# A hybrid layer on one core: attention's result carried by channels into gate and out projection

## The chip, the cores and the metric

The kernel runs on one core of a Trainium2 chip. The metric is the device time of one execution in microseconds (us), given as the median of the runs made on the same chip. All matrices and all arithmetic are float32.

## What is computed

Two layers follow each other on 2048 tokens of width 1024. The first one, which the change is in, is a hybrid: one wide input projection feeds a sliding-window attention (8 query heads, 2 key heads of width 64, blocks of 128 queries against 256 keys, one sink per head), an RWKV7 mixer and a gated linear attention (GLA). The three results, each times its gate, go side by side through one out projection. The second layer (top-k attention, pooling) is left out here; the change doesn't touch it.

```
s = einsum('bnqhgd,bnkhd->bnhgqk', qb, kb) * D ** -0.5 - slopes * dist     # masked
p = softmax(concatenate([s, sink], axis=-1), axis=-1)[..., :-1]
attn = einsum('bnhgqk,bnkhd->bnqhgd', p, vb) * silu(ag)
...
y = concatenate([attn, rwkv, gla], axis=-1) @ w_out
return x + gate[:, None] * rms_norm(y, g_post)
```

## The kernel before

The kernel has four stages, one after the other. Two of them matter here.

**First projections** (up to about 806 us). A loop over the 16 tiles of 128 tokens multiplies the normed tile by the columns of `w_in`. A helper `channels` gives a result with channels on the partitions (weights as the stationary side, 128 columns at a time), `tokens` one with tokens on the partitions (the tile as the stationary side, up to 512 columns at a time). The gate of attention, "ag", is the last product of a tile: `tokens(B[7], C_AG, 512)` at L380. ACT and DVE turn it into a gate and SP stores it with the rest of the tile. Its weights come by two DMAs (L215, `fetch_weights("ag", ...)`), those of the queries by 16 small ones (L211), which pick each head's 64 columns.

**Mixers** (about 808 to 1540 us, the `mixers` function, names with `b_`). A software pipeline over a pass number `p`: in one pass, tile `a = p + 1` gets its scores, attention, GLA and the inverse of RWKV's triangular matrix, tile `b = p` RWKV's state, tile `o = p - 1` the out projection (`dense`, in eight pieces), and `c = p + 2` its preparation. Each engine has its own list of steps, written out by hand in the loop at the end of its block, and goes through it strictly in order; waits are on semaphores. A ring of four PSUM banks is handed from user to user in the order of `bank_users`.

The steps that the change and the prediction speak of, for tile `a`:

- PE `scores` (L1047), two pairs of heads; DVE `biased` (L1470) adds the distance bias and keeps a maximum for each head; DVE `maxima` (L1477, L1478).
- ACT `probabilities` (L1260): eight exponentials with their sums in `den`, then the sinks' (L1263).
- PE `turn_probs` 0 to 3 (L1055) transposes two heads each, ACT and DVE copy them to `pT`; PE `attend` (L1065) multiplies by the values, which gives the result by channels, still not divided.
- ACT `take_attended` (L1273) copies it, PE `turn_attended` (L1072) transposes it to tokens by channels, DVE `attended` (L1518) divides it by `den` (whose `denominators`, L1511 and L1512, add the sink and take the reciprocal), POOL `attention_gate` (L836) multiplies by the gate.
- One pass later PE `turn_y` (L933) transposes all of `y` back to channels by tokens for the out projection: `turn_y(o, 1)` RWKV's and GLA's half, `turn_y(o, 0)` attention's; DVE (L1457) and ACT (L1209) copy them to `yT`; PE `dense` (L1115) multiplies.

Beside them run the five rounds of RWKV's inverse: PE `Z` (L979), ACT `take_Z` (L1219), PE `XY_products` (L989, L992), DVE `join_X` (L1429) and `join_Y` (L1433). DVE's `next_state` (L1447, L1450) makes the state that PE's `state_products` (L1011) reads. DVE's `gla_near` (L1483, L1495) takes GLA's first blocks out of the four ring banks; DVE's `out_sum` (L1562) finishes a tile of output. POOL's `level_distances` (L794), `key` (L773 to L775) and `bonus_terms` (L781, L782) prepare tile `c`; they begin when that tile's DMA has landed.

## Time and profile before

| | us |
|---|---|
| Median of 3 runs | 3612.84 |
| Lowest and highest | 3610.74, 3613.15 |
| The profiled execution | 3611.44 |
| Span of its trace | 3609.7 |

| Engine | busy us | share of the span |
|---|---|---|
| PE (matmul) | 3497.7 | 97% |
| PEld (weight load) | 2660.5 | 74% |
| DVE | 1910.8 | 53% |
| ACT | 1585.6 | 44% |
| POOL | 417.0 | 12% |

The span leaves out what lies before the first and behind the last instruction, here 1.7 us. An engine's busy share is taken over four stages that have different limits, so a stage's own rows decide. The granted clock of TensorE was 0.992 over the span.

### The profile page before, as it was taken

To read this page: it belongs to the slowest core of one execution; us is meant where nothing else is said; L and a number is where in the kernel's file an instruction comes from. 1 tells how busy PE (TensorE), PEld (TensorE's weight loads), DVE (VectorE), ACT (ScalarE), POOL (GpSimd) and SP (SyncE) were. 2 spreads that over 40 slices of the span, in tenths; PEclk is the share of its full clock that TensorE was granted. 3 is DMA by queue.
4 is the path that set the end of the run, shared out by engine and by line. 5 is a ranking of instruction groups with operands and counts; after the bars stand their busy time and mean duration, and the time that the engine had idled before them with its cause. 6 is when DMAs were issued, how large, how long until landed. Compare 5 with 4: busy or idle time off the path is not lost. (4 is left out here: it accounts for less than half of the span.)

```text
span 3609.7 us, 69211 instructions
## 1 busy us (share of the span) xinstructions
PE 3497.7 (97%) x28060; PEld 2660.5 (74%) x28060; DVE 1910.8 (53%) x4800; ACT 1585.6 (44%) x3591; POOL 417.0 (12%) x689
## 2 busy tenths in 40 slices
PE   6999999997999999989999999999999999999998
PEld 5887788766666666578778887777886677777765
DVE  5223333247777777534788788666683343333322
ACT  2223233323444444313677666777753344443320
POOL 0000000005444444310000000000000000000000
PEclk9999999998999999999999999999999999999999
DMA  9111111123222222241111114121215212111121
GB/s 314 54 54 48 54 54 54 54 86 147 84 77 81 76 76 76 90 132 48 50 54 62 53 52 168 56 66 60 69 46 194 74 53 78 42 49 67 48 84 41
DMA packets 134963, 282.05 MB, mean 78 GB/s; under 512 B 26640, under 2 KB 86048, under 8 KB 127136
## 3 DMA queue, kind: packets, MB, share of 16 engines
q1 hardware_dynamic: 125968, 267.75, 21.0%
q0 software_dynamic: 2304, 8.39, 0.6%
q8 instruction: 192, 3.15, 0.4%
q10 hardware_dynamic: 6416, 2.08, 0.2%
q14 instruction: 83, 0.68, 0.1%
HBM read 181.72 MB, written 96.47 MB: 77 GB/s over the span
## 5 line engine op out<-in xcount | busy, mean ns | idle before, releaser
L2575 ACT ACTIVATE at_pT<-at_bank 128x512 f32<-128x512 f32 (+3 forms) x320 | 154.4, 531 | 535.1 <-PE at_bank L2474 534.8
L1976 PEld LDWEIGHTS p_bank<-p_hT,w_in_rest 128*128 128x128 f32 x3072 | 345.5, 192 | 14.5 <-issue 12.4
L1976 PE MATMUL p_bank<-p_hT,w_in_rest 128*128 128x128 f32 x3072 | 350.2, 276 | 1.6 <-DVE p_st L2256 1.3
L2097 ACT ACTIVATE p_r<-p_acc,p_mid 128x384 f32<-128x384 f32 (+13 forms) x224 | 292.9, 1308 | 58.8 <-DVE p_acc L2283 54.4
L306 PE MATMUL p_bank<-p_hT,w_in_rest 128*128 128x128 f32 x2080 | 267.3, 275 | 0.0
L1115 PE MATMUL b_banks<-b_wout,b_yT 128*128 128x512 f32 x512 | 248.0, 610 | 3.7 <-DVE b_yT L1457 2.2
L306 PEld LDWEIGHTS p_bank<-p_hT,w_in_rest 128*128 128x128 f32 x2080 | 249.9, 192 | 0.0
L2515 PE MATMUL at_bank<-arena,at_y 128*128 128x512 f32 x512 | 239.8, 599 | 4.1 <-DVE at_y L2625 2.5
L1967 PE MATMUL p_bank<-arena,p_hT 128*128 128x512 f32 (+2 forms) x768 | 241.9, 467 | 1.3 <-ACT p_hT L2091 1.3
L2155 ACT ACTIVATE p_r<-p_bank,ahead_rows 128x512 f32<-128x512 f32 (+3 forms) x304 | 167.9, 635 | 156.5 <-PE p_bank L2070 144.5
L2058 PE MATMUL p_bank<-p_hTg,arena 128*128 128x256 f32 x1024 | 226.7, 381 | 1.7 <-ACT arena L2119 1.7
L2058 PE MATMUL p_bank<-p_hTg,w_in_rest 128*128 128x256 f32 x1024 | 228.2, 381 | 0.0
L2271 DVE SCALAR_TENSOR_TENSOR p_acc<-p_r,ahead_rows,p_acc 128x512 f32<-128x512 f32 (+3 forms) x266 | 166.9, 681 | 108.0 <-ACT p_r L2155 105.7
L2058 PEld LDWEIGHTS p_bank<-p_hTg,w_in_rest 128*128 128x128 f32 x1024 | 192.7, 190 | 42.0 <-issue 15.9
L2058 PEld LDWEIGHTS p_bank<-p_hTg,arena 128*128 128x128 f32 x1024 | 193.2, 190 | 39.6 <-issue 13.2
L2596 DVE CUSTOM_DVE_ANT_0 at_s<-at_bank,at_bias 128x512 f32<-128x512 f32 (+3 forms) x312 | 173.4, 608 | 71.9 <-PE at_bank L2461 67.8
L1967 PEld LDWEIGHTS p_bank<-arena,p_hT 128*128 128x128 f32 x768 | 142.3, 191 | 89.4 <-issue 69.1
L312 PE MATMUL p_bank<-w_in_rest,p_hT 128*128 128x512 f32 (+2 forms) x640 | 202.3, 463 | 0.0
L2289 DVE TENSOR_SCALAR_CACHE_REDUCE p_tie<-p_acc,p_mid 128x384 f32<-128x384 f32 (+13 forms) x126 | 186.3, 1479 | 14.7 <-ACT p_mid L2099 10.7
L306 PE MATMUL p_bank<-p_hT,arena 128*128 128x128 f32 x1248 | 175.6, 276 | 4.5 <-ACT p_hT L400 2.9
L312 PEld LDWEIGHTS p_bank<-w_in_rest,p_hT 128*128 128x128 f32 x640 | 110.4, 190 | 82.8 <-issue 76.5
L2439 POOL DMA_DIRECT2D out<-at_o x16 | 8.8, 549 | 1395.1 <-DVE at_o L2635 1395.1
(419 smaller groups left out, 6240.6 us busy)
## 6 DMA issues: line engine op xcount, KB each, us to landing
stage<-p_st SPq DMA_DIRECT2D x15, 1856.0 KB, 5.9
arena<-stage SPq DMA_DIRECT2D x15, 1856.0 KB, 7.5
at_rest<-stage SPq DMA_DIRECT2D x16, 1280.0 KB, 5.9
stage<-p_pr SPq DMA_DIRECT2D x128, 128.0 KB, 1.8
p_ada<-in_ada_w SPq DMA_DIRECT2D x8, 1024.0 KB, 9.2
p_xt<-in_x SPq DMA_DIRECT2D x16, 512.0 KB, 3.2
b_x<-in_x SPq DMA_DIRECT2D x16, 512.0 KB, 3.2
x<-b_x SPq DMA_DIRECT2D x16, 512.0 KB, 3.1
```

The lines of the kernel that those rows point to most:

```text
L306: last = mm(out, w_in(k, place(c), place(c) + P), hT[:, k, 1:P + 1], start=(k == 0), stop=(k == KD - 1))
L312: last = mm(out, hT[:, k, 1:P + 1], w_in(k, place(c), place(c) + width), start=(k == 0), stop=(k == KD - 1))
L1115: last = mm(OUT[:, :], yT[:, k, :], wout[:, k, half * 512:(half + 1) * 512], start=(k == 0), stop=(k == KD - 1))
L1967: last = mm(bank[:, 0:width], hTs[:, n % 2, k, :], weights(k, c, c + width), start=(k == 0), stop=(k == KD - 1))
L1976: last = mm(bank[:, m * P:(m + 1) * P], weights(k, c + m * P, c + (m + 1) * P), hTs[:, n % 2, k, :], start=(k == 0), stop=(k == KD - 1))
L2058: last = mm(gate_bank[:, 0:2 * P], weights(k, c, c + P), hTg[:, g % 2, k, :], start=(k == 0), stop=(k == KD - 1))
L2097: ch.link(f(flat(r[:, :, :])[:, 0:L], acc[:, slot.buf_a, 0:L], ACT.Sign, scale=-1.0, bias=m, accum_out=tally[:, 0:1]))
L2155: f(r[:, q, 0:width_], FRONT[q][:, 0:width_], ACT.Relu, scale=wi[:, slot.a, head:head + 1]).then_inc(S["relu_done"], 1)
L2271: last = stt(part, r[:, q, 0:width_], sgn, part, ALU.mult, ALU.add)
L2289: ch.link(ts(tie[:, 0:L], acc[:, slot.buf_b, 0:L], m[:, 0:1], 0.0, ALU.is_ge, ALU.add, accum_out=cnt[:, 0:1]))
L2515: last = mm(bank[:, :], y[:, k, :], wo[:, k, half * 512:(half + 1) * 512], start=(k == 0), stop=(k == KD - 1))
L2596: v.tensor_tensor_reduce(out=s[:, step % 2, g, at:at + w], in0=FRONT[2 * (j % 2) + g][:, 0:w], in1=bias_of(n)[:, at:at + w], scale=HEAD ** ...
```

## The change

Attention's result stays with channels on the partitions from `attend` to the out projection.

- `take_attended` writes it into `ys` as it is; POOL multiplies it there by a gate that now also has channels on its partitions; `dense` reads that half of its stationary side from `ys`. `turn_attended`, `turn_y(o, 0)`, ACT's copy of it and DVE's `attended` are gone. `dense` waits for attention's gate at its first piece and for the copy of the other half at its third.
- For this the gate "ag" is projected by `channels`, four times 128 columns, in the order in which heads lie in the attention's result. Its weights come by 16 DMAs like the queries', and the rows of `w_out` in the same order.
- The division moves to the probabilities: `denominators` now stands behind `gla_near`, ahead of `join_X(a, 1)`, and multiplies all of `s` by the reciprocals in two operations of 128 x 1024 elements each (for tile 0, 128 x 512). `turn_probs` waits for the first of them (0 and 1) or the second (2 and 3) instead of for ACT's exponentials.
- Around it: `maxima` goes ahead of `out_sum`; the first four exponentials go ahead of `take_Z(a, 1)`; `state_products(b, 1)` goes ahead of `turn_probs` 2 and 3; the ring has 26 users a pass instead of 28; for tile 0, `level_exps` and `scaled_levels` stand a little later.

```diff
@@ -212,7 +212,11 @@
...
                 sp.dma_start(xt[:, :], A["x"][0][P:2 * P, :]).then_inc(S["x_loaded"], 16)
-                fetch_weights("ag", (C_AG, C_RKV))
+                at = place(C_AG)
+                for k in range(KD):
+                    for g in range(A_KV):
+                        sp.dma_start(w_in(k, at, at + 512).rearrange("p (c g d) -> p g c d", g=2, d=HEAD)[:, g],
+                                     wsrc[:, k, C_AG + 256 * g:C_AG + 256 * g + 256].rearrange("p (c d) -> p c d", d=HEAD)).then_inc(S["ag_weights"], 16)
                 sp.wait_ge(S["first_added"], 2)
@@ -300,10 +304,11 @@
...
 
-                    def channels(out, c):
-
+                    def channels(out, c, more=0):
+
+                        at = place(c) + more
                         for k in range(KD):
-                            last = mm(out, w_in(k, place(c), place(c) + P), hT[:, k, 1:P + 1], start=(k == 0), stop=(k == KD - 1))
+                            last = mm(out, w_in(k, at, at + P), hT[:, k, 1:P + 1], start=(k == 0), stop=(k == KD - 1))
                         return last
@@ -378,8 +383,10 @@
...
                             last.then_inc(S["summed"], 1)
-                    pe.wait_ge(S["ag_weights"], 32)
-                    tokens(B[7][:, :], C_AG, 512).then_inc(S["ag_proj"], 1)
+                    pe.wait_ge(S["ag_weights"], 16 * A_KV * KD)
+                    for c in range(4):
+                        last = channels(B[7][:, c * P:(c + 1) * P], C_AG, c * P)
+                    last.then_inc(S["ag_proj"], 1)
 
@@ -680,9 +687,9 @@
...
             a, b, o = p + 1, p, p - 1
-            uses = [("x4t1", a), ("x4t0", a), ("yt1", o), ("yt0", o), ("gram0", a), ("gram1", a)] + [(f"score{i}", a) for i in range(4)]
+            uses = [("x4t1", a), ("x4t0", a), ("yt1", o), ("gram0", a), ("gram1", a)] + [(f"score{i}", a) for i in range(4)]
             uses += [("gla0", a)] * 4 + [(f"prob{i}", a) for i in range(4)] + [("rwkv", b), ("cum", p + 2), ("attT", a)] + [("gla1", a)] * 4
-            uses += [("ke", a), ("gout", a), ("att", a)]
+            uses += [("ke", a), ("gout", a)]
             bank_users += [(name, n) for name, n in uses if valid(n)]
@@ -727,7 +734,9 @@
...
                 wsrc = A["w_out"][0].rearrange("(k p) n -> p k n", p=P)
-                for k in range(0, KD, 2):
+                for g in range(A_KV):
+                    sp.dma_start(wout[half_of(g), 0:4, :], A["w_out"][0][256 * g:256 * g + 256, :].rearrange("(c d) n -> d c n", d=HEAD)).then_inc(S["wout_loaded"], 16)
+                for k in range(KD // 2, KD, 2):
                     sp.dma_start(wout[:, k:k + 2, :], wsrc[:, k:k + 2, :]).then_inc(S["wout_loaded"], 16)
@@ -830,7 +839,7 @@
...
                     y = ys[:, n % 3, 0:512]
-                    pool.wait_ge(S["att_taken"], n + 1)
+                    pool.wait_ge(S["attT_taken"], n + 1)
                     if n == 0:
@@ -922,16 +931,13 @@
...
 
-                def turn_y(n, e):
-                    if e == 0:
-                        pe.wait_ge(S["att_gated"], n + 1)
-                    else:
-                        pe.wait_ge(S["scaled_gla"], n + 1)
-                        pe.wait_ge(S["y_ready"], n + 1)
-                    bank = bank_for(f"yt{e}", n)
+                def turn_y(n):
+                    pe.wait_ge(S["scaled_gla"], n + 1)
+                    pe.wait_ge(S["y_ready"], n + 1)
+                    bank = bank_for("yt1", n)
                     for k in range(4):
-                        last = tr(bank[:, k * P:(k + 1) * P], ys[:, n % 3, (4 * e + k) * P:(4 * e + k + 1) * P], ident[:, :])
-                    last.then_inc(S[f"yt{e}_done"], 1)
+                        last = tr(bank[:, k * P:(k + 1) * P], ys[:, n % 3, (4 + k) * P:(5 + k) * P], ident[:, :])
+                    last.then_inc(S["yt1_done"], 1)
 
@@ -1048,7 +1054,7 @@
...
                 def turn_probs(n, j):
-                    pe.wait_ge(S[f"probs{j}"], n + 1)
+                    pe.wait_ge(S[f"probs{j // 2}"], n + 1)
                     bank = bank_for(f"prob{j}", n)
@@ -1064,13 +1070,6 @@
...
                     last.then_inc(S["attT_done"], 1)
-
-                def turn_attended(n):
-                    pe.wait_ge(S["attT_taken"], n + 1)
-                    bank = bank_for("att", n)
-                    for i in range(4):
-                        last = tr(bank[:, i * P:(i + 1) * P], flat(s[:, 0:2, :])[:, i * P:(i + 1) * P], ident[:, :])
-                    last.then_inc(S["att_done"], 1)
 
@@ -1105,14 +1104,16 @@
...
                     if piece == 0:
-                        for e in range(2):
-                            pe.wait_ge(S[f"yt{e}_taken"], n + 1)
+                        pe.wait_ge(S["att_gated"], n + 1)
                         if n == 0:
...
                         from_one(pe, S["r_taken"], 2 * n + half)
+                    if piece == 2:
+                        pe.wait_ge(S["yt1_taken"], n + 1)
                     for k in range(2 * (piece % 4), 2 * (piece % 4) + 2):
-                        last = mm(OUT[:, :], yT[:, k, :], wout[:, k, half * 512:(half + 1) * 512], start=(k == 0), stop=(k == KD - 1))
+                        part = ys[:, n % 3, k * P:(k + 1) * P] if k < 4 else yT[:, k - 4, :]
+                        last = mm(OUT[:, :], part, wout[:, k, half * 512:(half + 1) * 512], start=(k == 0), stop=(k == KD - 1))
                     if piece % 4 == 3:
@@ -1125,8 +1126,7 @@
...
                     if valid(o):
-                        turn_y(o, 1)
-                        turn_y(o, 0)
+                        turn_y(o)
                     if valid(a):
@@ -1154,11 +1154,11 @@
...
                         turn_probs(a, 1)
+                    if valid(b):
+                        state_products(b, 1)
+                    if valid(a):
                         turn_probs(a, 2)
                         turn_probs(a, 3)
-                    if valid(b):
-                        state_products(b, 1)
-                    if valid(a):
                         XY_products(a, 2)
@@ -1188,7 +1188,6 @@
...
                     if valid(a):
-                        turn_attended(a)
                         update_and_weights(a)
@@ -1202,11 +1201,6 @@
...
                         f(X4Ts[:, n % 2, 2 * e:2 * e + 2, :, :].rearrange("p a b c -> p (a b c)"), RING[spot_of[f"x4t{e}", n] % 4], ACT.Copy).then_inc(S[f"x4t{e}_taken"], 1)
-
-                def turned_y(n):
-                    act.wait_ge(S["yt0_done"], n + 1)
-                    from_one(act, S["out_done"], 2 * n)
-                    f(flat(yT[:, 0:4, :]), bank_of("yt0", n), ACT.Copy).then_inc(S["yt0_taken"], 1)
 
@@ -1250,16 +1244,13 @@
...
 
-                def probabilities(n, j):
-                    if j == 2:
-                        act.wait_ge(S["max_ready"], n + 1)
-                        from_one(act, S["att_taken"], n)
+                def exponentials(n, g):
+                    act.wait_ge(S["max_ready"], n + 1)
+                    from_one(act, S["probs1"], n)
                     first = 0 if n else P
-                    for e in range(2):
-                        h = 4 * (j % 2) + 2 * (j // 2) + e
-                        last = f(s[:, h, first:], s[:, h, first:], ACT.Exp, bias=nm[:, h:h + 1], accum_out=den[:, h:h + 1])
-                    last.then_inc(S[f"probs{j}"], 1)
-                    if j == 3:
+                    for h in range(4 * g, 4 * g + 4):
+                        f(s[:, h, first:], s[:, h, first:], ACT.Exp, bias=nm[:, h:h + 1], accum_out=den[:, h:h + 1])
+                    if g == 1:
                         f(am[:, :], am[:, :], ACT.Exp).then_inc(S["sink_exp"], 1)
@@ -1270,7 +1261,8 @@
...
                     act.wait_ge(S["attT_done"], n + 1)
-                    f(flat(s[:, 0:2, :]), bank_of("attT", n), ACT.Copy).then_inc(S["attT_taken"], 1)
+                    from_one(act, S["out_done"], 2 * (n - 2))
+                    f(ys[:, n % 3, 0:512], bank_of("attT", n), ACT.Copy).then_inc(S["attT_taken"], 1)
 
@@ -1310,20 +1302,17 @@
...
                 decays(0)
-                level_exps(0)
                 for p in range(-1, TILES + 1):
...
                         turned_X4(a)
-                    if valid(o):
-                        turned_y(o)
+                    if a == 0:
+                        level_exps(a)
                     if valid(a):
                         first_X(a)
+                        exponentials(a, 0)
                         take_Z(a, 1)
-                        probabilities(a, 2)
-                        probabilities(a, 0)
-                        probabilities(a, 1)
-                        probabilities(a, 3)
+                        exponentials(a, 1)
                     if valid(o):
@@ -1462,7 +1451,6 @@
...
                         from_one(dve, S["sink_exp"], n)
-                        from_one(dve, S["att_done"], n)
                     first = 0 if n else P
@@ -1510,13 +1498,11 @@
...
                     ch.link(v.reciprocal(den[:, :], den[:, :]))
-
-                def attended(n):
-                    dve.wait_ge(S["att_done"], n + 1)
-                    from_one(dve, S["yt0_done"], n - 2)
-                    by_pair = lambda ap: ap.rearrange("p (g i d) -> p i g d", g=2, d=HEAD)
-                    tt(by_pair(ys[:, n % 3, 0:512]), bank_of("att", n).rearrange("p (i g d) -> p i g d", g=2, d=HEAD),
-                       spread(den[:, :].rearrange("p (g i) -> p i g", g=2).unsqueeze(3), [P, 4, 2, HEAD]), ALU.mult).then_inc(S["att_taken"], 1)
+                    first = 0 if n else P
+                    for i in range(2):
+                        by_group = s[:, :, first:].rearrange("p (g i e) t -> p i g e t", g=2, i=2)[:, i]
+                        share = spread(den[:, :].rearrange("p (g i e) -> p i g e", g=2, i=2)[:, i].unsqueeze(3), [P, 2, 2, 2 * P - first])
+                        tt(by_group, by_group, share, ALU.mult).then_inc(S[f"probs{i}"], 1)
 
@@ -1565,7 +1551,6 @@
...
                 bonus(0)
-                scaled_levels(0)
                 dve.wait_ge(S["setup_done"], 1)
@@ -1575,20 +1560,22 @@
...
                         take_grams(a)
+                        if a == 0:
+                            scaled_levels(a)
                         biased(a, 0)
                         biased(a, 1)
+                        maxima(a)
                     if valid(o - 1):
...
                     if valid(a):
-                        maxima(a)
                         gla_near(a)
+                        denominators(a)
                         join_X(a, 1)
...
                         turned_probs(a, 1)
-                        denominators(a)
                     if valid(b):
@@ -1624,7 +1611,6 @@
...
                     if valid(a):
-                        attended(a)
                         gla_scale(a)
...
```

DVE, in the full pass for tile 2 of the mixers, from `gla_near` on (before):

```order
L1483 TENSOR_TENSOR b_gA<-b_banks,ident 128x512
L1495 COPY_PREDICATED b_gA<-b_g_masks,b_banks 128x256
L1495 COPY_PREDICATED b_gA<-b_g_masks,b_banks 128x128x2
L1495 COPY_PREDICATED b_gA<-b_g_masks,b_banks 128x64x4
L1429 TENSOR_TENSOR b_XY<-b_XY,b_banks 128x256
L1447 SCALAR_TENSOR_TENSOR b_dM<-b_banks,b_pend,b_pair 128x128 x2
L1450 SCALAR_TENSOR_TENSOR b_M<-b_M,b_pend,b_dM 128x128 x2
L1433 TENSOR_TENSOR b_XY<-b_XY,b_banks 128x256
L1507 COPY b_pT<-b_banks 128x512
L1511 TENSOR_TENSOR b_den<-b_den,b_am 128x8
L1512 RECIPROCAL b_den<-b_den 128x8
L1438 SCALAR_TENSOR_TENSOR b_SA<-b_banks,b_U 64x256
```

The same place after the change (L1471 and L1483 are `gla_near`, L1505 the two wide multiplications, L1418 `join_X`, L1436 and L1439 `next_state`, L1422 `join_Y`):

```order
L1471 TENSOR_TENSOR b_gA<-b_banks,ident 128x512
L1483 COPY_PREDICATED b_gA<-b_g_masks,b_banks 128x256
L1483 COPY_PREDICATED b_gA<-b_g_masks,b_banks 128x128x2
L1483 COPY_PREDICATED b_gA<-b_g_masks,b_banks 128x64x4
L1499 TENSOR_TENSOR b_den<-b_den,b_am 128x8
L1500 RECIPROCAL b_den<-b_den 128x8
L1505 TENSOR_TENSOR arena<-arena,b_den 128x2x512 x2
L1418 TENSOR_TENSOR b_XY<-b_XY,b_banks 128x256
L1436 SCALAR_TENSOR_TENSOR b_dM<-b_banks,b_pend,b_pair 128x128 x2
L1439 SCALAR_TENSOR_TENSOR b_M<-b_M,b_pend,b_dM 128x128 x2
L1422 TENSOR_TENSOR b_XY<-b_XY,b_banks 128x256
L1495 COPY b_pT<-b_banks 128x512
```

`denominators` and the two wide operations have moved from behind the copy of the probabilities to ahead of `join_X`, `next_state` and `join_Y`.

PE, the same pass, from the fourth piece of `dense` to the second round's products (before):

```order
L1115 MATMUL b_banks<-b_wout,b_yT 128x512 x2
L1055 MATMUL b_banks<-ident,arena 128x128 x4
L979 MATMUL b_banks<-b_XY,b_cT 64x64 x8
L1055 MATMUL b_banks<-ident,arena 128x128 x12
L1011 MATMUL b_banks<-b_M,b_WT 64x128 x2
L989 MATMUL b_banks<-b_Z,b_XY 64x64 x8
```

The same place after (L1116 is `dense`, L1061 `turn_probs`, L985 `Z`, L1017 `state_products`, L995 and L998 the products):

```order
L1116 MATMUL b_banks<-b_wout,b_yT 128x512 x2
L1061 MATMUL b_banks<-ident,arena 128x128 x4
L985 MATMUL b_banks<-b_XY,b_cT 64x64 x8
L1061 MATMUL b_banks<-ident,arena 128x128 x4
L1017 MATMUL b_banks<-b_M,b_WT 64x128 x2
L1061 MATMUL b_banks<-ident,arena 128x128 x8
L995 MATMUL b_banks<-b_Z,b_XY 64x64 x8
L998 MATMUL b_banks<-b_XY,b_Z 64x64 x8
```

The state's products stand between the second and the third group of transposes, so that these have four transposes before and eight behind them instead of twelve before.

## Rows read from the trace of the kernel before

**Rows 1.** The mixers' stage by windows: length, busy us of each engine (instructions), TensorE clock

```profile
850.00:1500.00 650.00, 640.68 (x8857) 440.94 (x8857) 478.95 (x1265) 272.09 (x988) 303.92 (x447) 1.00 0.21 73
```

**Rows 2.** Timeline of PE, one full pass: start, length, line, operation, count [idle before]

```profile
1196.07 1.04 PE L922 MATMUL b_banks<-ident,b_X 128*128 128x128 f32 x8
...
1197.62 1.09 PE L933 MATMUL b_banks<-ident,b_y 128*128 128x128 f32 x8
...
1213.90 0.60 PE L1055 MATMUL b_banks<-ident,arena 128*128 128x128 f32 x4
1214.43 0.68 PE L979 MATMUL b_banks<-b_XY,b_cT 64*64 64x64 f32 x16
1215.04 1.53 PE L1055 MATMUL b_banks<-ident,arena 128*128 128x128 f32 x12
1216.51 0.65 PE L1011 MATMUL b_banks<-b_M,b_WT 128*64 128x128 f32 x4
1217.09 0.68 PE L989 MATMUL b_banks<-b_Z,b_XY 64*64 64x64 f32 x16
...
1236.46 0.60 PE L1072 MATMUL b_banks<-ident,arena 128*128 128x128 f32 x4
...
1239.65 1.04 PE L922 MATMUL b_banks<-ident,b_X 128*128 128x128 f32 x8
```

**Rows 3.** Timeline of PE, first projections, one tile

```profile
404.97 0.83 PE L306 MATMUL p_bank<-p_hT,arena 128*128 128x128 f32 x6
...
406.75 0.83 PE L306 MATMUL p_bank<-p_hT,arena 128*128 128x128 f32 x6
...
414.20 2.74 PE L312 MATMUL p_bank<-arena,p_hT 128*128 128x512 f32 x6
...
421.07 0.83 PE L306 MATMUL p_bank<-p_hT,arena 128*128 128x128 f32 x6
```

**Rows 4.** Timeline of DVE, the same pass as rows 2

```profile
1192.03 1.08 DVE L1404 TENSOR_TENSOR b_gql<-b_ge,arena 128x896 f32<-128x896 f32 x1
...
1209.22 0.69 DVE L1483 TENSOR_TENSOR b_gA<-b_banks,ident 128x512 f32<-128x512 f32 x1 [0.72 <-PE b_banks L1085]
1209.95 1.97 DVE L1495 COPY_PREDICATED b_gA<-b_g_masks,b_banks 128x256 f32<-128x256 uint32 x3
1212.27 0.42 DVE L1429 TENSOR_TENSOR b_XY<-b_XY,b_banks 128x256 f32<-128x256 f32 x1 [0.34 <-PE b_banks L992]
...
1213.24 1.10 DVE L1450 SCALAR_TENSOR_TENSOR b_M<-b_M,b_pend,b_dM 128x128 f32<-128x128 f32 x2
...
1216.35 0.16 DVE L1511 TENSOR_TENSOR b_den<-b_den,b_am 128x8 f32<-128x8 f32 x1
```

**Rows 5.** Timeline of ACT, the same pass

```profile
1208.54 0.51 ACT L1260 ACTIVATE arena<-arena,b_nm 128x256 f32<-128x256 f32 x1
...
1212.49 0.19 ACT L1263 ACTIVATE b_am<-b_am 128x8 f32<-128x8 f32 x1
```

**Rows 6.** Timeline of POOL, the same pass

```profile
1207.65 2.64 POOL L794 TENSOR_TENSOR b_ge<-arena 128x128 f32<-128x128 f32 x7 [1.92 <-DMA arena<-stage]
1210.26 0.72 POOL L773 TENSOR_TENSOR arena<-arena,ahead_rows 128x256 f32<-128x256 f32 x1
...
1213.47 0.73 POOL L782 TENSOR_TENSOR arena<-arena,ahead_rows 128x256 f32<-128x256 f32 x1
```

**Rows 7.** Timeline of all engines, the last passes of the mixers

```profile
1503.93 0.61 POOL L818 TENSOR_TENSOR b_t<-b_late,b_bonus 128x256 f32<-128x256 f32 x1
1504.06 1.57 DVE L1562 SCALAR_TENSOR_TENSOR b_x<-b_r,b_osum,b_x 128x1024 f32<-128x1024 f32 x1 [0.73 <-issue]
...
1504.62 1.58 POOL L819 TENSOR_TENSOR b_t<-b_t,b_rows 128x256 f32<-128x256 f32 x1
...
1524.21 7.11 PE L1115 MATMUL b_banks<-b_wout,b_yT 128*128 128x512 f32 x16 [1.27 <-DVE b_yT L1457]
```

**Rows 8.** Timeline of SP's queue, first projections

```profile
59.34 6.27 SPq L211 DMA_DIRECT2D w_in_rest<-in_w_in  x10
```

8 lines of the change are left out of this document (4 added, 4 removed).

## The prediction

> **What bounds the kernel now.** I read the stages first. In the mixers PE is busy 640.7 of 650 us at full clock, DVE 479, POOL 304 [rows 1], and in the timeline of one full pass PE's rows stand without a bracket of idle time, from one pass start at 1196.07 to the next at 1239.65, 43.58 us [rows 2]. So there PE's own work sets the time, and any wait put into it adds in full. The first projections look the same: the rows of one tile follow each other without a bracket [rows 3]. What has to be found is what PE loses in work, and whether something that PE reads now comes after PE wants it. For the second I read DVE, ACT and POOL in the same pass [rows 4 to 6]. All times of day below are those of this pass.
>
> **What PE loses and gains.** Four transposes before `Z` of round 2 take 1214.43 - 1213.90 = 0.53 us, the twelve behind it 1216.51 - 1215.04 = 1.47, so 0.49 for four; `turn_y` has eight, and its row has 1.09 [rows 2]. `turn_attended` (four, at 1236.46) and half of `turn_y` (four, at 1197.62) go: about 1.03 us a pass, the first 0.5 of it near the pass's start. The out projection keeps its multiplications, only half of its operand is read elsewhere: nothing.
>
> The gate "ag" by tokens takes 421.07 - 414.20 = 6.87 us; a block of 128 channels takes 406.75 - 404.97 = 1.78, four take 7.12 [rows 3]. That is +0.25 us a tile, **+4.0** for 16 tiles, all of it on PE's path.
>
> The 16 small loads of its weights: ten such loads held SP's queue for 6.27 us [rows 8], 0.63 each, so 16 take 10 us where two were. Behind them on SP are the loads of the ada weights and the next x tile. The gate is the last product of the first tile and the query loads went ahead of it in the same way; I take 0 and keep 0 to 5 us (half of the 10) for the range.
>
> ACT loses a copy and DVE a multiplication of 512 elements from PSUM; neither is on the path. POOL's gate waited for DVE's division, now for ACT's copy, which is earlier; it has other work in front of it in its list, so nothing.
>
> **What DVE gets ahead of PE's next step.** `Z` of round 2 started at 1214.43 and needs `join_X` of round 1, which ran from 1212.27 to 1212.69: 1.74 us of slack [rows 2, 4]. After the change PE wants it 0.5 earlier, at 1213.93, and DVE does this first:
>
> - `gla_near` began at 1209.22, released by PE, and ended at 1209.95 + 1.97 = 1211.92 [rows 4]. It moves with PE: 1208.7 to 1211.4. The sinks' exponential is no hindrance: ACT needed 1208.54 to 1212.68 for all [rows 5] and starts about 1.6 us earlier, since `maxima` no longer stands behind `out_sum` (1.57 us, of which 0.48 is waiting, in [rows 7]) and PE is 0.5 ahead.
> - the sum and the reciprocal of `den`: the first has 0.16 [rows 4], the second and the two semaphores between them I put at 0.25: 0.4, to about 1211.85.
> - two wide multiplications. No row has this operation on 1024 elements with both inputs in SBUF; the nearest is 1.08 us for 896 [rows 4], scaled 1.2, with 1.15 from start to start. Together 2.3, the bounds are 2.0 and 2.6.
> - `join_X`, 0.42.
>
> If nothing else interferes, `join_X` begins at 1214.15 and ends at 1214.55, and `Z` is 0.65 late. The state follows: `next_state` (0.6 and two operations of `L1450`, 0.65 when free) would be ready at 1215.8, the state's products, now moved ahead, begin then, 0.58 and eight transposes (0.98) later comes round 2's first product at 1217.4 instead of 1217.09. That is +0.35 against the gain of 0.5 that should have been there, and with `turn_attended` gone the pass is 0.15 us **shorter**.
>
> **The pair of engines.** It won't be free, I think. POOL runs `level_distances` from 1207.65, when the tile's DMA lands, and then five multiplications of 256 elements, the first at 1210.26, the last at 1213.47 to 1214.20, each 0.72, 0.80 apart [rows 6]. What happens when DVE and POOL both read two operands from SBUF stands in three places. `L1450`, two operations on 128 elements, took 1.10 us under POOL's last one and ended at 1214.34, 0.14 behind it [rows 4, 6]. In the last passes `L1562` (1024 elements, DVE) was issued at 1504.06 within a POOL operation that ended at 1504.54; it ended at 1505.63, 1.09 behind it. The POOL operation issued at 1504.62 took 1.58 and ended 0.57 behind DVE's [rows 7]. One waits for the other, and they take turns.
>
> The Trainium skill has this as a rule (SBUF — State Buffer, Who interferes with whom): a tensor_tensor on VectorE with both inputs in SBUF and a GpSimd instruction that reads SBUF exclude each other, and the second one fully blocks. By the rows the later one loses a little less than its full length; by the rule taken to the letter both wide operations and the POOL operations beside them pay in full, some 0.5 us more a pass, and the time would be about 3637 as an estimate by that page.
>
> With turns taken by the rows: POOL's five operations come 0.5 later, like the gate on which its DMA waits, at 1210.8, 1211.6, 1212.4 and on. The first wide operation, issued at 1211.85, waits until 1212.3 and ends 1.09 later at 1213.4; POOL's third ends at 1213.95; the second wide one at 1215.05; `join_X` runs 1215.0 to 1215.4. `Z` waits from 1213.93 to 1215.4, **1.5 us**. Then `L1447` to 1215.9, `L1450` behind POOL's fifth until 1216.85; the state's products begin at 1216.9; round 2's product 1.56 later, at 1218.45. Against 1217.09 that is +1.35, less 0.5 for `turn_attended`: **+0.8 us a pass**. The transposes themselves aren't what waits: the first wide result is there at 1213.4, PE wants it at 1213.4.
>
> **Sum.** Tiles 2 to 14 have a full pass with POOL's preparation: 13 x 0.8 = +10.4. Tile 15 has no tile to prepare: -0.15. Tile 1 has no out projection beside it that covers DVE's chain, so all of the inserted 2.7 and a collision or two land there, less 0.5: +3. Tile 0 has half the width: +1.5. In the last two passes the out projection waited for the copies, once for 1.27 us [rows 7]; now it can begin without them: -1.6 with the transposes. The gate's projection +4.0. Together +17.2 on the profiled 3611.4, that is 3628.6; the median of the runs shown stands 1.4 above that execution: **3630 us**.
>
> **The rivals.**
>
> - *No collision*: POOL is through, or DVE gets the pair between POOL's operations without loss. Per pass -0.15, tile 1 +2, tile 0 +1, last passes -1.6, gate +4.0: +3.3, so 3616. For it: the start of POOL's five hangs on a DMA, and 0.5 us of slip is my inference. Against: they cover 3.9 us, and a shift of one microsecond either way still meets a wide operation.
> - *Faster*: PE waits for none of it. Then 16 x 1.03 = 16.5 goes, 4.0 comes: 3600. The place is `Z` of round 2, and the price is DVE's 2.7 us in front of `join_X`. It decides the other way only if that chain starts 0.65 us earlier than I have it (and the pair is free); `gla_near` is released by PE's GLA products, which the change moves only with all the rest. Little speaks for it but the wide operations being shorter than 0.9 each, which the 1.08 for 896 elements denies.
> - *Dearer*: collisions also on `den` itself, full lengths, and the first tile's weights late. 1.5 a pass x 13 = 19.5, with tile 0 and 1 +5, gate +4, weights +4, tail -1.6: +31, so 3644.
> - *The gate's cost is hidden or the order of weights costs nothing* changes 4 us at most and none of the above.
>
> **Chances.** Forecast with collisions 0.5, no collision 0.22, dearer 0.13, faster 0.15. The range 3608 to 3643 takes in the second and most of the third. A difference of 0.2% (7.2 us) is about what a measurement of this kernel can tell from none: faster by that only in the fourth case, 0.15; the no-collision case lies within it, 0.22; the rest is slower, 0.63.
>
> **What the profile of the changed kernel would show.** PE in a full pass: a bracket of 1 to 2 us ahead of `Z` of round 2, released by DVE's `join_X`, and a smaller one ahead of the state's products; no bracket ahead of `turn_probs`. Pass length 44.4 (43.4 without collisions, 42.5 if the faster case holds). DVE: the wide operations at 1.5 to 1.9 us each instead of 1.2, `L773`'s successors on POOL longer than 0.72. First projections: a tile 0.25 longer. I am wrong if the wide operations show 1.2 us and PE still waits, if the bracket stands at `turn_probs` (then ACT's sums are the late part), or if the transposes were not worth 0.5 each.

## The result and the profile after

| | before | after |
|---|---|---|
| Median | 3612.99 us (4 runs) | 3653.39 us (4 runs) |
| Lowest and highest | 3610.74, 3613.18 | 3648.51, 3654.25 |
| The profiled execution | 3611.44 | 3653.63 |
| Span of its trace | 3609.7 | 3651.8 |

The ratio is 1.0112 [1.0099, 1.0125]: 40 us slower. The sign of the prediction held, the size did not: 17 us were forecast, and the range ended at 3643.

```profile
850.00:1500.00 650.00, 610.27 (x8293) 412.13 (x8293) 485.94 (x1216) 253.17 (x927) 311.32 (x425) 0.97 0.20 72
```

PE is busy 30 us less than in [rows 1] and its mean clock is 0.97, so PE both waits more and runs slower in part of the time. What PE waits for between 900 and 1500 us (line and what it waited for, us in total, times, longest):

```profile
PE b_banks L985 <- DVE b_XY L1418: 18.0, 14, 1.3
PE b_banks L1017 <- DVE b_M L1439: 6.5, 13, 0.8
PE b_banks L1061 <- DVE arena L1505: 1.7, 6, 0.3
```

The first is `Z` of round 2, the second the state's products, the third `turn_probs`. Timeline of PE in one full pass, the answer to [rows 2]:

```profile
1183.72 1.04 PE L931 MATMUL b_banks<-ident,b_X 128*128 128x128 f32 x8
...
1199.29 1.98 PE L1116 MATMUL b_banks<-b_wout,b_yT 128*128 128x512 f32 x4
1201.59 0.66 PE L1061 MATMUL b_banks<-ident,arena 128*128 128x128 f32 x4 [0.32 <-DVE arena L1505]
1203.58 0.68 PE L985 MATMUL b_banks<-b_XY,b_cT 64*64 64x64 f32 x16 [1.34 <-DVE b_XY L1418]
1204.20 0.66 PE L1061 MATMUL b_banks<-ident,arena 128*128 128x128 f32 x4
1205.15 0.62 PE L1017 MATMUL b_banks<-b_M,b_WT 128*64 128x128 f32 x4 [0.29 <-DVE b_M L1439]
1205.70 1.09 PE L1061 MATMUL b_banks<-ident,arena 128*128 128x128 f32 x8
1206.72 0.68 PE L995 MATMUL b_banks<-b_Z,b_XY 64*64 64x64 f32 x16
```

Three brackets stand where [rows 2] has none. Timeline of DVE in the same pass ([rows 4] before):

```profile
1196.43 0.69 DVE L1471 TENSOR_TENSOR b_gA<-b_banks,ident 128x512 f32<-128x512 f32 x1 [0.82 <-PE b_banks L1084]
1197.16 1.96 DVE L1483 COPY_PREDICATED b_gA<-b_g_masks,b_banks 128x256 f32<-128x256 uint32 x3
1199.15 0.52 DVE L1499 TENSOR_TENSOR b_den<-b_den,b_am 128x8 f32<-128x8 f32 x1
...
1199.95 3.25 DVE L1505 TENSOR_TENSOR arena<-arena,b_den 128x1024 f32<-128x1024 f32 x2
1203.12 0.41 DVE L1418 TENSOR_TENSOR b_XY<-b_XY,b_banks 128x256 f32<-128x256 f32 x1
...
1204.09 0.91 DVE L1439 SCALAR_TENSOR_TENSOR b_M<-b_M,b_pend,b_dM 128x128 f32<-128x128 f32 x2
```

Timeline of POOL in the same pass ([rows 6] before):

```profile
1198.92 0.73 POOL L782 TENSOR_TENSOR arena<-arena,ahead_rows 128x256 f32<-128x256 f32 x1
1199.73 0.72 POOL L783 TENSOR_TENSOR arena<-arena,b_rows 128x256 f32<-128x256 f32 x1
1200.53 1.59 POOL L784 TENSOR_TENSOR arena<-arena 128x256 f32<-128x256 f32 x1
1202.20 1.59 POOL L790 TENSOR_TENSOR arena<-arena 128x256 f32<-128x256 f32 x1
```

The two take turns, as forecast. `L783` holds the pair until 1200.45. The first wide operation, issued at 1199.95, ends at about 1201.55 (an estimate: `turn_probs`, which waits for it, starts at 1201.59); `L784` ends at 1202.12, the second wide one near 1203.2, `L790` at 1203.79. Each DVE operation ends 1.1 us behind POOL's, each POOL operation 0.57 behind DVE's, the two numbers of [rows 7]. The Trainium skill's exclusive lock (SBUF — State Buffer, Who interferes with whom) fits this in its order, and in the rows the one that waited ends 0.1 to 0.2 us less than its full length behind the other (DVE's takes 1.22 alone, POOL's 0.73).

Now the clock, in the pass that follows, in windows of the changed kernel:

```profile
1240.00:1250.00 10.00, 8.33 (x110) 4.99 (x106) 8.94 (x14) 5.46 (x22) 7.62 (x12) 1.00 0.40 141
1250.00:1254.00 4.00, 3.44 (x26) 2.81 (x28) 2.55 (x5) 0.06 (x1) 0.27 (x1) 0.60 0.00 0
1254.00:1258.00 4.00, 4.00 (x86) 3.40 (x82) 2.11 (x7) 0.71 (x2) 0.85 (x1) 0.97 0.00 0
```

and PE's timeline there:

```profile
1248.46 0.68 PE L985 MATMUL b_banks<-b_XY,b_cT 64*64 64x64 f32 x16 [1.34 <-DVE b_XY L1418]
...
1250.56 0.82 PE L1017 MATMUL b_banks<-b_M,b_WT 128*64 128x128 f32 x4 [0.83 <-DVE b_M L1439]
1251.31 1.97 PE L1061 MATMUL b_banks<-ident,arena 128*128 128x128 f32 x8
1253.21 1.12 PE L995 MATMUL b_banks<-b_Z,b_XY 64*64 64x64 f32 x16
```

After the waits the clock falls to the lower level, and the eight transposes take 1.97 us instead of 1.09. That pass lasts 46.95 us, its neighbours about 45. The wait for the state is 0.83 us here and was 0.29 in the pass above; it is 0.83 in every third pass or so, where `L1439` takes 1.45 us beside POOL.

**Where the 42.2 us between the profiled executions are**, by the starts of the passes (PE's first transposes of a pass, as at the top of [rows 2]):

| | before | after | difference | forecast |
|---|---|---|---|---|
| The first pass of the mixers starts at | 816.55 | 820.74 | +4.2 | +4.0 |
| Tile 0 | 35.69 | 42.93 | +7.2 | +1.5 |
| Tile 1 | 37.11 | 42.69 | +5.6 | +3 |
| Tile 2 | 45.24 | 48.90 | +3.7 | +0.8 |
| Tiles 3 to 14 | 12 x 43.58 | 547.2 | +24.2 | +9.6 |
| From tile 15's start to the next stage | 90.2 | 88.7 | -1.4 | -1.75 |
| The second layer | | | -1.3 | 0 |

Of the twelve passes eight last 44.6 to 45.6 us and four, with the lower clock in them, 46.2 to 47.1. At 45.0 each, +1.4 a pass, they make 17.0; the other 7.2 belong to the four with the clock. Of these some 5.5 are the clock itself: three of the four had the long wait for the state too, and the one pass with the same waits and no fall took 45.59, where they took 46.95 to 47.06.

### The profile page after: what moved, and what is told of

Its sections match the earlier page's. It is cut to its first block and busy times, and to the rows that moved or that the text cites. A ratio compares the mean times of both kernels' runs of the same rounds, so it can differ in the third digit from the quotient of the medians.

```text
span 3651.8 us, 70471 instructions
## 1 busy us (share of the span) xinstructions
PE 3509.4 (96%) x28700; PEld 2722.1 (75%) x28700; DVE 1942.3 (53%) x4816; ACT 1575.4 (43%) x3575; POOL 439.4 (12%) x689
## 5 line engine op out<-in xcount | busy, mean ns | idle before, releaser
L1962 PEld LDWEIGHTS p_bank<-p_hT,w_in_rest 128*128 128x128 f32 x3072 | 345.4, 192 | 14.0 <-issue 12.4
L1962 PE MATMUL p_bank<-p_hT,w_in_rest 128*128 128x128 f32 x3072 | 349.9, 276 | 1.3 <-DVE p_st L2242 1.3
L311 PE MATMUL p_bank<-p_hT,w_in_rest 128*128 128x128 f32 x2720 | 349.2, 275 | 0.0
L311 PEld LDWEIGHTS p_bank<-p_hT,w_in_rest 128*128 128x128 f32 x2720 | 326.4, 192 | 0.0
L311 PE MATMUL p_bank<-p_hT,arena 128*128 128x128 f32 x1632 | 228.9, 276 | 4.3 <-ACT p_hT L407 2.9
L311 PEld LDWEIGHTS p_bank<-p_hT,arena 128*128 128x128 f32 x1632 | 204.7, 192 | 8.0 <-issue 4.7
L2460 PEld LDWEIGHTS at_bank<-ident,at_s 128*128 128x128 f32 x1088 | 126.0, 141 | 43.9 <-issue 37.2
L2621 DVE TENSOR_TENSOR at_o<-at_bank,at_o 128x512 f32<-128x512 f32 x32 | 22.1, 692 | 252.3 <-PE at_bank L2501 252.3
```

The costliest lines, as they stand in the source:

```text
L311: last = mm(out, w_in(k, at, at + P), hT[:, k, 1:P + 1], start=(k == 0), stop=(k == KD - 1))
L1962: last = mm(bank[:, m * P:(m + 1) * P], weights(k, c + m * P, c + (m + 1) * P), hTs[:, n % 2, k, :], start=(k == 0), stop=(k == KD - 1))
L2460: last = tr(TURNED[j % 2][:, e * P:(e + 1) * P], s[:, step % 2, g, at + e * P:at + (e + 1) * P], ident[:, :])
```

## Experiments

The numbers of passes are those of tile 0, tile 1, tile 2 and one full pass. Before has 35.69, 37.11, 45.24 and 43.58 us, the changed kernel 42.93, 42.69, 48.90 and 44.6 to 47.1. They come from one profiled execution of each kernel. Full passes of one kernel without a fall of the clock lie within about 1 us of each other, in most versions within 0.5; tile 0 varies more, as two kernels below show whose edits first act in a later pass: with the changed kernel's program for tile 0, one took 40.16 us for it and the other 43.93.

### POOL out of the way

```diff
                         level_distances(c)
+                        if valid(b):
+                            pool.wait_ge(S["M_ready"], 2 * b + 1)
                         key(c)
```

> The changed kernel, with POOL's key and bonus of the next tile made to wait until DVE's next_state of the first chunk is done, so that no POOL operation stands beside the two wide multiplications. If the collisions between DVE and POOL stretch them (theory): the wide operations take 1.2 us each instead of 1.4 to 1.8, PE's wait ahead of the second Z falls from 1.3 to about 0.7 us, a full pass takes 43.6 to 43.9 us instead of 45.1 to 47.0, and the time is about 3627 us (3633 if TensorE's clock still falls in some passes). If the wide operations are slow by themselves (rival: the broadcast operand): they stay at 1.6 to 1.8 us and the time at 3653.

Measured: 3625.85 us, ratio 1.0043 [1.0026, 1.0060]; passes 40.16 (tile 0, which the edit doesn't reach), 40.6, 45.52 and 43.6 to 43.8, at full clock from tile 2 on. DVE's timeline in a full pass:

```profile
1225.27 2.36 DVE L1507 TENSOR_TENSOR arena<-arena,b_den 128x1024 f32<-128x1024 f32 x2
1227.54 0.41 DVE L1420 TENSOR_TENSOR b_XY<-b_XY,b_banks 128x256 f32<-128x256 f32 x1
```

and PE's, the only bracket left there:

```profile
1228.01 0.68 PE L987 MATMUL b_banks<-b_XY,b_cT 64*64 64x64 f32 x16 [0.78 <-DVE b_XY L1420]
```

The wide operations alone take 2.36 us for the pair (2.3 was the estimate), with POOL beside them 3.25. The collisions and what they bring in clock are worth some 26 of the 40 us, of which up to 2.8 may be tile 0's scatter.

### Without the wide operations

```diff
...
-                        tt(by_group, by_group, share, ALU.mult).then_inc(S[f"probs{i}"], 1)
+                        v.tensor_copy(nm[:, 4 * i:4 * i + 4], den[:, 4 * i:4 * i + 4]).then_inc(S[f"probs{i}"], 1)
```

> The changed kernel without the two wide multiplications: the probabilities stay undivided, two copies of four elements stand in their place, and the result isn't divided at all. Theory: PE's waits in the full passes go, a pass takes 42.6 us, no pass has the clock at half, and the time is about 3606 us; that would confirm the 1.03 us a pass that the transposes were worth. Rival (the waits come from other parts of the new order, such as maxima or the state's products ahead of the transposes): passes stay above 44 us and the time above 3630.

Measured: 3612.77 us, ratio 1.0003 [0.9994, 1.0013]; passes 40.04, 40.33, 45.14 and 42.9 to 43.1. So the 40 us go with the two wide operations, and even with the division free the change gives nothing. A full pass gains 0.5 to 0.7 us instead of 1.03, and tiles 0 and 1 lose 4.3 and 3.2 us with no wide operation in them.

### Is it the wait that lowers the clock?

```diff
                         turn_probs(a, 0)
+                        if valid(o):
+                            for _ in range(9):
+                                tr(ZB[:, 0:P], ident[:, :], ident[:, :])
                         Z(a, 2)
```

> The changed kernel with nine transposes of the identity into an unused part of Z's bank put on PE ahead of the second Z in each full pass, about 1.1 us of work in a wait of 1.3. Their result is overwritten. Theory (the falls of TensorE's clock in some passes come from PE's wait there): the passes of 47 us turn into 45.1, none has the clock at half, time about 3644 us. Rival (the clock falls for another reason, or the filler only adds to the path): 3653 us or more.

Measured: 3646.91 us, ratio 1.0099 [1.0082, 1.0116]; full passes 44.6 to 45.6, none with the lower clock. PE's waits:

```profile
PE b_banks L1017 <- DVE b_M L1442: 6.2, 12, 0.8
PE b_banks L985 <- DVE b_XY L1421: 5.2, 14, 0.5
```

DVE's part is as in the changed kernel, only PE does useless work in the wait, and the passes above 46 us are gone. One run without falls is unlikely to be luck: three other kernels below have the waits of the changed one in their full passes ("The start of tile 0 as before", "The gate by tokens", the changed kernel with plain loads), and each fell three or four times. The falls of the clock follow from the wait itself. The long wait for the state matters too: in tiles 2 to 14 of the changed kernel and these three the clock fell in 11 of the 20 passes where it was 0.83 us and in 4 of the other 32. Here it was 0.83 in five passes, and none fell.

### The start of tile 0 as before

`level_exps(0)` and `scaled_levels(0)` back ahead of the loop:

```diff
                 decays(0)
+                level_exps(0)
...
-                    if a == 0:
-                        level_exps(a)
...
                 bonus(0)
+                scaled_levels(0)
...
-                        if a == 0:
-                            scaled_levels(a)
```

> The changed kernel with tile 0's level_exps and scaled_levels back ahead of the loop, where they stood before the change. In the changed kernel the first of scaled_levels' operations took 3.24 us beside POOL's lower_levels, and tile 0's pass 42.9 us instead of 35.7. Theory: some 5 us of these 7.2 come from that move, so tile 0's pass is about 38 us and the time about 3648. Rival (tile 0 is late by the wide operations and by the clock that is at half until then): its pass stays at 42 us or more and the time at 3653.

Measured: 3651.77 us, ratio 1.0105 [1.0088, 1.0122]; tile 0 39.72, tile 1 41.67. The full passes fell to the lower clock four times again, and the total doesn't differ from the changed kernel's beyond the intervals. What the edit undoes stands in the changed kernel's timeline of DVE in tile 0:

```profile
826.62 1.29 DVE L1405 TENSOR_TENSOR b_G<-b_banks,b_tri 128x512 f32<-128x512 f32 x2 [5.69 <-DMA b_alibi<-in_k_alibi]
...
829.02 3.24 DVE L1393 TENSOR_TENSOR b_gql<-b_ge,arena 128x896 f32<-128x896 f32 x1
...
832.59 0.34 DVE L1458 CUSTOM_DVE_ANT_0 arena<-b_banks,b_alibi,b_sinks 128x128 f32<-128x128 f32 x1
```

The scaling left the idle 5.69 us and took 3.24 (1.1 alone) beside a POOL operation, ahead of the bias. Before, the first bias stood at 826.15, 9.6 us behind the start of the pass; in the changed kernel it is 11.9 behind it, with the scaling back 9.6 again. That this shortens the pass isn't shown: with POOL out of the way the first bias came 13.0 behind the start, later than in the changed kernel, and the pass took 40.16, not 42.93. What differs among the kernels with this tile 0 is how long the lower clock lasts. The windows from 846 to 856 us, in this order: the changed kernel, POOL out of the way (same tile 0), PE filled from tile 2 on (same tile 0), the start as before:

```profile
846.00:856.00 10.00, 9.15 (x116) 6.80 (x112) 3.60 (x10) 2.66 (x8) 1.03 (x1) 0.56 0.25 100
846.00:856.00 10.00, 8.44 (x187) 6.80 (x187) 6.13 (x17) 3.58 (x11) 1.03 (x1) 1.00 0.39 156
846.00:856.00 10.00, 9.14 (x104) 6.92 (x104) 3.87 (x11) 2.28 (x7) 1.03 (x1) 0.50 0.27 106
846.00:856.00 10.00, 8.44 (x173) 6.61 (x169) 5.85 (x16) 3.57 (x11) 1.03 (x1) 0.95 0.31 121
```

With 0.50 and 0.56 there, tile 0 took 42.93 and 43.93 us, with 0.95 and 1.00 it took 39.72 and 40.16.

### The division late

`turn_probs` moves behind `rwkv_out`, all its transposes in one row, and the wide operations behind `next_state` and `join_Y`, with the start as before; the ring and ACT's and DVE's lists follow that order. PE's part of the edit:

```diff
                     if valid(a):
-                        turn_probs(a, 0)
                         Z(a, 2)
-                        turn_probs(a, 1)
                     if valid(b):
                         state_products(b, 1)
                     if valid(a):
-                        turn_probs(a, 2)
-                        turn_probs(a, 3)
                         XY_products(a, 2)
                     if valid(b):
                         rwkv_out(b)
                     if valid(a):
+                        turn_probs(a, 0)
+                        turn_probs(a, 1)
+                        turn_probs(a, 2)
+                        turn_probs(a, 3)
                         Z(a, 3)
```

> The changed kernel with the same work in another order. DVE divides the probabilities behind join_X and join_Y of round 1, next_state and addition of the second chunk, and takes RWKV's centre right behind; PE turns the probabilities behind RWKV's output, just ahead of the third Z; RWKV's output has its place in the ring ahead of them; tile 0's level_exps and scaled_levels are back ahead of the loop. Theory (what costs is that DVE's 2.4 us stand in front of join_X while POOL wants the same ports): POOL's five operations are over by then, PE has 4 us of other work, no clock falls in the full passes, a pass takes 42.9 us or less (as the undivided kernel) and the time is about 3605 us. Rival (the work is simply too late for attend or for join_X of round 3, and PE waits there): passes of 43.6 us or more, 3618 us or more.

Measured: 3617.42 us, ratio 1.0013 [1.0004, 1.0022]; passes 37.03, 39.58, 45.15 and 43.43. Some 35 of the 40 us are a question of order: of where the division stands above all, since this version still has the wide operations, and in part of the transposes in one row and the old start. What is left of waiting for `M` between 900 and 1500 us:

```profile
PE b_banks L1017 <- DVE b_M L1438: 2.8, 10, 0.4
```

### The gate by tokens

```diff
-                    for c in range(4):
-                        last = channels(B[7][:, c * P:(c + 1) * P], C_AG, c * P)
-                    last.then_inc(S["ag_proj"], 1)
+                    tokens(B[7][:, :], C_AG, 512).then_inc(S["ag_proj"], 1)
```

> The changed kernel with the gate projected by tokens and its weights in two loads, as before the change; the gate is then multiplied in the wrong layout. If the gate's cost is PE's 0.25 us a tile and the 16 small loads cost nothing: the first pass of the mixers begins 4.0 to 4.2 us earlier than in the changed kernel and the time is about 3649. If the small loads delay something too: more than 5 us.

Measured: 3649.41 us in one execution; the first pass starts at 816.6 instead of 820.7. The weights come by two loads again. All kernels with the gate by channels start that pass at 819.9 to 821.5, the three with it by tokens at 816.2 to 816.7. So the 4.0 us of the gate are right within that scatter, and its 16 small loads cost nothing that shows.

### The transposes in one group

Without the wide operations, `turn_probs` 1 to 3 again ahead of the state's products:

```diff
                         turn_probs(a, 1)
+                        turn_probs(a, 2)
+                        turn_probs(a, 3)
                     if valid(b):
                         state_products(b, 1)
                     if valid(a):
-                        turn_probs(a, 2)
-                        turn_probs(a, 3)
```

> The undivided kernel (no wide multiplications, result not divided) with the state's products behind all twelve transposes of the probabilities, as before the change. Its passes took 42.86 us where 42.55 were expected. If each group of transposes that stands alone costs PE about 0.1 us to enter: the pass falls to about 42.75. If the state's products are what costs there: no change.

Measured: 3609.05 us in one execution; passes 39.32, 39.99, 44.38 and 42.71. So the eight transposes are worth 0.87 us a pass, and cutting a row of twelve in two took 0.15 to 0.36 of it back. What is left of `turn_y`, in a full pass of this version:

```profile
1201.75 0.66 PE L939 MATMUL b_banks<-ident,b_y 128*128 128x128 f32 x4
1202.34 1.10 PE L952 MATMUL b_banks<-b_X4T 64*64 64x128 f32 x32
```

The four take 0.59 us to the next row, where eight took 1.02 (1198.64 less 1197.62), so four fewer save 0.43 and not half.

### The late division with POOL behind it

```diff
+                        if valid(a):
+                            pool.wait_ge(S["probs1"], a + 1)
                         key(c)
```

> The version with the late division and the old start, and GpSimd's key and bonus terms of the next tile begin only when VectorE's second wide multiplication has ended, so that no VectorE operation of the middle of the pass has one of GpSimd's beside it. Theory (the last wait of that version, 0.4 us a pass for next_state's 1.50 us beside GpSimd, goes with the collision): no wait of TensorE for M, full passes of 43.43 - 0.4 = 43.0 us, 3617 - 13 x 0.4 = about 3612 us, the time of the kernel before within 0.1%. Rival (GpSimd is then late itself: kk_length and the lower levels come behind and VectorE or ScalarE waits for them): passes stay at 43.4 us or grow, with a new wait for a GpSimd line, 3617 us or more.

Measured: 3613.99 us, ratio 1.0008 [0.9999, 1.0017]; passes 38.29, 39.35, 44.96 and 43.29. The wait for `M` is gone; it was 0.4 us at most, and 2.8 in total, 0.2 a pass on average. Of this 0.12 came back (43.41 to 43.29 on average), and a new wait stands in its place, 3.0 us in 13 passes: `turn_probs` needs a bank that DVE empties late. PE's timeline in a full pass:

```profile
1224.20 1.53 PE L1063 MATMUL b_banks<-ident,arena 128*128 128x128 f32 x12
1225.96 0.63 PE L1063 MATMUL b_banks<-ident,arena 128*128 128x128 f32 x4 [0.24 <-DVE b_t L1514]
```

### What is lost in the first two passes

Without the wide operations, grouped, and with the start of before (the edits above):

> The kernel whose attention result is not divided (the wide multiplications are left out) and whose twelve transposes stand in one group, with the levels' exponentials and the scaling of tile 0 back ahead of the first pass. If the moved scaling of tile 0 is what the first pass loses, that pass goes from 39.3 to about 36.5 us (35.7 in the kernel before), tile 1's pass stays near 40, the full passes at 42.7, and the time is 3609 - 2.8 = about 3606 us, 6 us under the kernel before. If the first pass loses it elsewhere (the lower clock that follows a start without work ready), it stays at 38 us or more and the time at 3608 to 3609 us.

Measured: 3606.76 us, ratio 0.9988 [0.9979, 0.9997]; passes 40.07, 39.77, 44.37, 42.71. The time is that of the first case, but the pass decides, and it is the second's: with the scaling back this version's tile 0 is no shorter than without (39.32), though 1.6 us of it are a bracket of the kind told further down. Next, PE kept busy in these two passes, in the late version with POOL behind it and in the kernel before. The edit puts 38 transposes of the identity into the first pass and 33 into the second (not 43 and 38, as the expectations say):

```diff
+                def fill(p, count):
+                    if p < 1:
+                        for _ in range(count):
+                            tr(OUT[:, 0:P], ident[:, :], ident[:, :])
...
+                        fill(p, 12 if p < 0 else 5)
                         grams(a)
                         scores(a, 0)
+                        fill(p, 3)
```

> The version with the late division, the old start and GpSimd's preparation behind the second wide multiplication, and in the mixers' first two passes (which have no out projection) TensorE transposes the identity matrix into an unused bank where it waits: 43 transposes in the first pass, 38 in the second, whose results nobody reads. Theory (most of what tiles 0 and 1 lose against the kernel before is the longer stretch at the lower clock that follows the waits): the 41 us at the lower level shrink to about 15, the two passes go from 38.3 and 39.35 to about 36 and 37, and the time from 3614.0 to about 3610 us. Rival (VectorE's and GpSimd's chains set the first passes, whatever TensorE's clock): the passes stay at 38 and 39 us or grow by the fillers, and the time stays at 3614 us or above.

> The kernel before with the same 43 and 38 filling transposes at the same waits of its first two passes: what the fillers do by themselves. Its passes are 35.7 and 37.1 us with 27 and 3 us at the lower level; with the theory they shrink by 1 to 3 us in all (about 3610 us), with the rival nothing changes or they grow (3612 to 3614 us). The difference between this kernel's first two passes and those of the other filled one is what the change costs there without the clock: the theory says 1 us or less, the rival 4 to 5 us.

Measured: the late version 3615.35 us, ratio 1.0012 [1.0002, 1.0022], passes 37.66 and 37.25; the kernel before 3608.01, ratio 0.9990 [0.9980, 0.9999], passes 33.7 and 35.57. The first two passes as windows, first the kernel before:

```profile
816.00:896.00 80.00, 63.15 (x1063) 52.08 (x1064) 57.65 (x154) 34.70 (x121) 39.57 (x54) 0.86 0.35 133
```

The changed kernel:

```profile
816.00:896.00 80.00, 57.09 (x811) 46.01 (x813) 52.19 (x127) 25.44 (x87) 36.75 (x50) 0.67 0.48 146
```

The late division with POOL behind it:

```profile
816.00:896.00 80.00, 60.13 (x954) 49.37 (x954) 56.09 (x147) 31.34 (x106) 36.71 (x53) 0.77 0.47 144
```

The same filled:

```profile
816.00:896.00 80.00, 63.98 (x1054) 52.32 (x1056) 57.97 (x150) 32.64 (x117) 37.96 (x54) 0.89 0.50 148
```

The kernel before, filled:

```profile
816.00:896.00 80.00, 70.63 (x1187) 57.36 (x1189) 60.93 (x164) 34.82 (x121) 43.05 (x56) 0.98 0.38 140
```

The clock, 0.86 before, was 0.67 in the changed kernel; with the filling it is 0.89 and 0.98. The filling shortens the late version's two passes by 0.6 and 2.1 us, and those of the kernel before by 2.0 and 1.5. So the clock costs both kernels something, but it isn't what sets them apart: the late version's two passes are 4.8 us longer than those of the kernel before without the filling and 5.6 with it, 4.0 in tile 0 and 1.7 in tile 1. That is the rival's number (4 to 5) and more, and the late version's time didn't fall (3613.99 at 1.0008 before, 3615.35 at 1.0012 now). Was it the order of Z and the exponentials?

```diff
+                        if a < 2:
+                            take_Z(a, 1)
                         exponentials(a, 0)
-                        take_Z(a, 1)
+                        if a > 1:
+                            take_Z(a, 1)
```

> The filled version with the late division, and for tiles 0 and 1 ScalarE takes Z of round 1 ahead of the first four exponentials, as the kernel before does; from tile 2 on the order of the change stays. In the first two passes the exponentials wait for the maxima, which come after Z is done, so that Z stood behind them: it was taken 2.3 us after its products in tile 0 and 3.5 us after them in tile 1 (0.7 to 1.3 us in the kernel before). If this order is what the change costs in the first two passes, they go from 37.7 and 37.25 to about 36 and 36 us, and the time from 3615 to about 3612 us. If not, only the wait's place changes (TensorE then waits for VectorE, the bias and the maxima or the late tile load of GpSimd), the passes stay within 0.5 us and the time at 3614 to 3615 us.

Measured: 3614.36 us, ratio 1.0002 [0.9993, 1.0012]; tile 0 40.13, tile 1 37.18. No: ACT takes Z 1.5 us earlier in tile 0's pass and PE waits elsewhere. But tile 0's pass is 2.5 us longer, and 2.0 of it is the growth of a bracket that nothing in the profile releases (1.73 us in the filled version). It stands in the middle of eight filling transposes that follow each other in the program without a wait:

```profile
837.44 0.76 PE L922 MATMUL b_banks<-ident 128*128 128x128 f32 x5
841.94 0.55 PE L922 MATMUL b_banks<-ident 128*128 128x128 f32 x3 [3.74 <-issue]
```

and its windows have an odd pair of numbers at the end, DMA engines busy throughout and little moved:

```profile
830.00:840.00 10.00, 7.59 (x140) 6.29 (x140) 8.05 (x31) 4.33 (x20) 4.97 (x8) 1.00 1.04 208
```

The kernel before moves 341 GB/s in that window and is done by 840. The difference is in the loads of `w_out`: the change brings its first half, to have the rows in heads' order, by two loads that reach 64 partitions each. Three kernels test this. The loads as before, in the filled version with Z first, and in the changed kernel:

```diff
-                for g in range(A_KV):
-                    sp.dma_start(wout[half_of(g), 0:4, :], A["w_out"][0][256 * g:256 * g + 256, :].rearrange("(c d) n -> d c n", d=HEAD)).then_inc(S["wout_loaded"], 16)
-                for k in range(KD // 2, KD, 2):
+                for k in range(0, KD, 2):
```

> The filled version that takes Z first in tiles 0 and 1, but the first half of w_out comes as in the kernel before, by two loads over all 128 partitions instead of two over 64 partitions each (the rows are then not in the order of the attention's result; attention's part of the output is another). In the changed kernels those two loads keep the DMA engines full for some 15 us at 205 to 230 GB/s where the kernel before moves 390 to 460, until about 848 instead of 840, and TensorE has a gap of 1.7 to 3.7 us in tile 0's pass that nothing in the profile releases. Theory (TensorE waits for its own instructions, whose fetch stands behind those loads, and VectorE's and GpSimd's data come late for the same reason): the gap goes and tile 0's pass falls from 40.1 to 36.5 us or less, the time from 3614.4 to about 3610 us. Rival (the gap has another cause, the loads are off the path): the pass stays at 38 to 40 us.

> The changed kernel with the first half of w_out loaded as in the kernel before (the same remark on its output), nothing else. If the slow loads cost the changed kernel's first pass as they do in the filled version, that pass falls from 42.9 by 1 to 4 us and the time from 3653 to about 3650 us; if there the late start of the scaling and the lower clock are all, it stays at 42.5 to 43 us and the time at 3653 us.

And the halves by turns, in the filled version:

```diff
-                for g in range(A_KV):
-                    sp.dma_start(wout[half_of(g), 0:4, :], A["w_out"][0][256 * g:256 * g + 256, :].rearrange("(c d) n -> d c n", d=HEAD)).then_inc(S["wout_loaded"], 16)
+                for c in range(4):
+                    for g in range(A_KV):
+                        at = 256 * g + HEAD * c
+                        sp.dma_start(wout[half_of(g), c, :], A["w_out"][0][at:at + HEAD, :]).then_inc(S["wout_loaded"], 16)
```

> The filled version that takes Z first, with the first half of w_out in eight loads of 64 rows that go by turns to the lower and the upper 64 partitions, so that the order of the rows stays that of the change and the whole result is computed. If the low rate comes from a load that reaches only 64 partitions at a time, alternating pieces of 256 KB bring it back to 350 GB/s or more and this version runs like the one with the plain loads, near 3610 us. If each load is slow by itself, or the six more issues (about 0.6 to 0.8 us each on SyncE's queue) cost as much, it stays at 3614 us.

Measured: plain loads in the filled version 3611.46 us, ratio 0.9997 [0.9987, 1.0007], tile 0 33.89 (from 40.13), no such bracket; in the changed kernel 3650.85, ratio 1.0110 [1.0092, 1.0128], tile 0 40.32 (from 42.93); halves by turns 3611.72, ratio 0.9997 [0.9987, 1.0007], tile 0 35.87, still with brackets of 1.42 and 1.14. The 6.2 us of tile 0 are more than its scatter, but the medians moved less, by some 2 us against the kernel before, and the two profiled executions (3616.31 and 3609.26) lie at opposite ends of their kernels' ranges. The same window with the plain loads, in the filled version:

```profile
830.00:840.00 10.00, 8.93 (x176) 7.50 (x176) 8.08 (x30) 4.71 (x21) 5.21 (x9) 1.00 1.03 415
```

And with halves by turns:

```profile
830.00:840.00 10.00, 8.47 (x159) 6.94 (x155) 8.16 (x31) 4.33 (x20) 4.98 (x8) 1.00 1.05 244
```

The loads that reach 64 partitions run at about half the rate and fill the DMA engines all the same. The Trainium skill has the rule (SBUF — State Buffer, Door 1: The DMA port swizzle): partitions 0 to 63 reach 8 of the 16 ports, some 218 GB/s at most. The trace agrees: this window shows 211 in the changed kernel, 213 in the late version with POOL behind it and 208 here. In all the kernels with these loads it is 199 to 225, the two values above 218 in windows that can hold parts of other loads too. Splitting and alternating the halves gave 244, not 415.

What these loads hold up is shown only in part. Brackets like this stand in tile 0 of four kernels, all with the slow loads (the three filled ones and the undivided one with the old start), and in none with plain loads. But nine other kernels with the slow loads, the changed one among them, have none. So the changed kernel's tile 0 didn't lose its time by such a bracket, and its 40.32 with plain loads is what the same tile 0 took with the slow ones in another run (40.16): a gain there isn't shown. That TensorE waits for its own instructions behind the loads is my guess, and no run shows it directly.

## Why the prediction was right in its mechanism and wrong in its size

- **What bounds the kernel, and where the wait falls: right.** The largest bracket stands at `Z` of round 2, released by `join_X`: 1.34 us against 1.5. The smaller one ahead of the state's products is there too: 0.29 in most passes, where the times of day worked out leave some 0.4. The turns of DVE and POOL run as worked out, the wide pair takes 3.25.
- **The gate: right**, +4.2 against +4.0.
- **Without collisions** I had 43.4 us a pass; POOL out of the way gave 43.6 to 43.8.
- **Wrong, the worth of the transposes.** I took 1.03 us; without the wide operations 0.5 to 0.7 showed (0.65 on average), 0.87 with the transposes in one row. The reading error: `turn_y`'s eight take 1.09 in [rows 2], so four were put at half; the remaining four take 0.66. What a short row costs to enter stays, and the new cut in the row of twelve was costed at nothing. Over tiles 2 to 14 this term is 5 us.
- **A little too small, the waits.** The state's products wait 0.83 us in every third pass or so, and `turn_probs`, where no bracket was forecast, up to 0.3 in about half of them. Mean waiting is (18.0 + 6.5 + 1.7) / 13 = 2.0 us a pass, where the times of day worked out have 1.9. With 0.65 gained this gives nearly +1.4, what the eight passes without a fall show, where the sum had +0.8. The smaller gain is most of that difference.
- **Wrong by omission, the clock.** The text says that PE runs at full clock and that a wait "adds in full". It adds more: the clock falls after it in some passes. In tiles 3 to 14 that is some 5.5 us by the passes with the same waits and no fall, 6.5 by the filled version, and in tile 2 another 1.4 to 2 (48.90 against 46.86 to 47.52 in the four kernels with these waits, or with PE filled, and no fall there). This term, put at nothing, is the largest of those that failed in the full passes: some 7 us of the 17.5 that tiles 2 to 14 took beyond the sum.
- **Wrong, tiles 0 and 1: +7.2 and +5.6 against +1.5 and +3, the cause open.** Without the wide operations they still lost 4.3 and 3.2, so much of it isn't the division. Some 3 of tile 0's 7.2 are scatter that goes with how long the lower clock lasts. Two costs in the diff had no price in the sum, the moved scaling, which took 3.24 us and put the first bias 2.3 later, and `w_out`'s two loads at half the rate; neither is shown to have made the changed kernel's pass longer. For the loads I weighed the gate's 16 small ones, which cost nothing, and not these two. The late version with the old start and the slow loads lost 1.3 and 2.5, so most of both passes' loss goes with the order; which part of the order isn't separated.
- **The rivals.** "No collision" and "faster" were excluded by the first rows. "Dearer" had 3644 from full lengths of the lock and late weights; it was nearer in time, but for other reasons.

No version with the division beats the kernel before. The best with the whole result, late division with POOL behind it, filled first passes, Z first in them and halves by turns, equals it, and the kernel before with the same filling is 0.1% faster (3608.01, ratio 0.9990): 0.87 us saved a pass is met by 4 us for the gate and what the division costs wherever it stands, some 0.6 us a pass in its best place (43.29 against 42.71).

## What to carry to other kernels

Ahead of a step that a full engine waits for, an operation costs its length, the other engine's turn on the shared pair, and at times the clock after the wait; put the division behind the chain that the full engine needs, which with the transposes in one row gave back some 35 of 40 us here. When a diff moves work out of idle time or reshapes a load, price it in the pass in which there is no cover: the first one. Read a group's fixed part before halving its time, and look at how many partitions each load reaches. Before a difference in one pass of one execution is given a cause, look at a kernel in which that pass is the same.

## What the runs showed of the hardware

- A wait of 1.34 us and one of 0.83 shortly behind it (1248.46 and 1250.56), in a stage otherwise full, was followed by the lower clock in 11 of 20 passes of four kernels; with 0.3 or less as the second wait in 4 of 32. With nine idle transposes in the first wait, which left 0.36 of it, it never was, in 13 passes. In the changed kernel a fall made the pass some 1.2 to 1.5 us longer.
- Transposes of 128 x 128: 16 in two groups took 2.00 us without what stands between the groups, in three groups 2.14 to 2.37.
- While loads into 64 partitions ran, 199 to 225 GB/s were moved at a DMA share of 1.02 to 1.05, with loads into 128 in their place 412 and 415 at 1.02 and 1.03.
- Operations of DVE on 1024 elements from SBUF took 1.22 us each alone (2.36 the pair), 1.75 with POOL's beside them (both medians; 3.25 the pair shown); POOL's on 256 elements 0.73 alone, 1.59 beside them.
